# Two-layer diffusion trunk on one core: w_out half loaded during the RWKV recurrence, expert weights in 512 KB pieces, second expert product transposed

## The reference

```python
mix = concat([mla_o, hg_o, rw_o]) @ w_out                    # 1024 x 1024
x   = layernorm(ALPHA * x + g1 * mix) * ln_g[0] + ln_b[0]
h2  = x * (1 + sc2) + sh2
aff = softmax(h2 @ router)                                   # 16 experts
gate, idx = top_k(aff.T, cap)     # per expert: 64 sample tokens, 16 prompt tokens
xe  = h2[idx]
he  = silu(xe @ w1) * (xe @ w3)                              # 1024 -> 1024, twice
ye  = (he @ w2) * gate                                       # 1024 -> 1024
ffn = zeros.at[idx].add(ye)
x   = layernorm(ALPHA * x + g2 * ffn) * ln_g[1] + ln_b[1]
```

## Time and profile before

| | before |
|---|---|
| median of 3 runs | 3464.21 us (3459.65 to 3464.31) |
| the profiled execution, its own time | 3468.49 us |
| its span, first to last instruction | 3466.6 us |
| mean granted TensorE clock | 0.907 of full speed |
| TensorE busy (matmul) | 2812.5 us, 81% of the span |
| VectorE, ScalarE, GpSimd busy | 1260.2, 519.7, 753.1 us |
| moved by DMA | 533.90 MB, mean 154 GB/s |
| expert weight issues (SP) | 128 of 2048 KB, 128 of 1024 KB |

### The profile page before, as it was taken

One profiled execution on the slowest core, in us unless ns is written; L12 is line 12 of the kernel. 1 busy time (PEld: TensorE's weight loads), 2 busy tenths in 40 slices (PEclk: granted clock), 3 DMA queues, 4 the chain that ended last, 5 costly groups with the idle time before them and its releaser, 6 DMA issues. The chain is left out here.

```text
span 3466.6 us, 72945 instructions
## 1 busy us (share of the span) xinstructions
PE 2812.5 (81%) x32720; PEld 1898.1 (55%) x32720; DVE 1260.2 (36%) x2711; ACT 519.7 (15%) x1001; POOL 753.1 (22%) x874
## 2 busy tenths in 40 slices
PE   5998884648584999999979988566585859999995
PEld 1555554538534766666425645355474446666662
DVE  1101668774524111111240036786754331111114
ACT  0102331131101000000010022302211100100101
POOL 0000908343220000000010037272430200000102
PEclk9999996869896999999989999878798879999998
DMA  8300000000052988888661000000003259899972
GB/s 349 129 20 36 1 8 4 2 7 3 3 218 104 387 332 333 338 341 345 254 260 62 2 36 1 9 3 7 2 3 113 118 212 359 342 350 349 349 291 79
DMA packets 68854, 533.90 MB, mean 154 GB/s; under 512 B 12704, under 2 KB 14560, under 8 KB 32192
## 3 DMA queue, kind: packets, MB, share of 16 engines
q1 hardware_dynamic: 65472, 518.75, 38.5%
q0 software_dynamic: 3072, 10.49, 1.1%
HBM read 520.43 MB, written 8.78 MB: 153 GB/s over the span
## 5 line engine op out<-in xcount | busy, mean ns | idle before, releaser
L2276 PEld LDWEIGHTS ps<-arena 128*64 128x64 f32 x16384 | 580.7, 138 | 93.2 <-issue 90.6
L2276 PE MATMUL ps<-arena 128*64 128x80 f32 x16384 | 601.5, 235 | 20.5 <-issue 11.7
L2289 PE MATMUL ps<-arena 128*128 128x512 f32 (+1 forms) x1024 | 472.8, 606 | 4.6 <-ACT arena L2339 4.6
L527 PE MATMUL ps<-arena 128*128 128x128 f32 (+1 forms) x1088 | 294.7, 434 | 4.6 <-DVE arena L580 4.6
L2404 DVE TENSOR_TENSOR arena<-arena,ps 128x32 f32<-128x32 f32 (+1 forms) x192 | 45.1, 263 | 686.0 <-ACT arena L2347 686.0
L2289 PEld LDWEIGHTS ps<-arena 128*128 128x128 f32 (+1 forms) x1024 | 165.2, 171 | 221.3 <-issue 210.4
L527 PEld LDWEIGHTS ps<-arena 128*128 128x128 f32 x1088 | 164.3, 191 | 135.1 <-issue 130.1
L2034 POOL DMA_INDIRECT arena<-h_d,arena x32 | 39.3, 1227 | 800.1 <-DVEq L2371 662.8
L2347 ACT ACTIVATE arena<-ps 128x160 f32<-128x160 f32 x128 | 38.9, 304 | 944.0 <-PE ps L2276 944.0
L2384 DVE TENSOR_TENSOR arena<-arena,ps 128x512 f32<-128x512 f32 x140 | 96.2, 687 | 206.1 <-PE ps L2305 158.2
L1982 PE MATMUL ps<-arena 128*128 128x512 f32 x320 | 141.4, 605 | 25.1 <-DMA arena<-in_w_out 25.1
(11 more groups left out here) (347 smaller groups left out, 4152.9 us busy)
## 6 DMA issues: line engine op xcount, KB each, us to landing
arena<-in_ex_w SPq DMA_DIRECT2D x128, 2048.0 KB, 8.7
arena<-in_ex_w SPq DMA_DIRECT2D x128, 1024.0 KB, 7.6
arena<-in_ada_w SPq DMA_DIRECT2D x24, 2048.0 KB, 13.7
arena<-in_w_t SPq DMA_DIRECT2D x34, 512.0 KB, 3.4
arena<-in_w_out SPq DMA_DIRECT2D x4, 2048.0 KB, 10.3
arena<-in_w_tok SPq DMA_DIRECT2D x2, 3712.0 KB, 17.4
h_d<-x_sb SPq DMA_DIRECT2D x10, 512.0 KB, 2.6
arena<-mod_d SPq DMA_DIRECT2D x8, 512.0 KB, 10.8
```

Source lines behind the costliest of these rows:

```text
L527: i = nc.tensor.matmul(ps[:, n % 8, 0:c1 - c0], ring[:, a % WRING, k, :], e.hT[:, k, c0:c1], start=k == 0, stop=k == KD - 1)
L2276: m = nc.tensor.matmul(gated(j)[c * 64:(c + 1) * 64, f, a, :], w13[:, j, a, k, f * P + c * 64:f * P + (c + 1) * 64], xT[:, x % 2, k, :], s ...
L2289: m = nc.tensor.matmul(ps[0:CAP if x % 2 == 0 else P, 4 + h, :], rows[x % 2][:, f, :], w2[:, (f // 2 + 2) % 4, f % 2, h * 512:(h + 1) * 51 ...
```

## The change

- `w_out` is laid out on the host as [layer, row, half, k, 512]. Its first half is loaded in two pieces by SP within the RWKV phase, after the factor stage (`xy`) and into parts of the arena that the rest of that phase doesn't use (`first_half`). The second half is the first instruction of SP's output program, ahead of `clear_last`.
- A `w1`/`w3` quarter is loaded by four DMAs and a quarter of `w2` by two, each of 512 KB with 4 KB to a partition. There are six slots of 2 MB (`WG`) and four of 1 MB (`WP`). Five quarters are loaded in the output phase; the sixth and four of `w2` in the route phase.
- `project(x, j)` now has `w2` as the stationary side in 128x64 tiles and the 80 tokens as the moving side: 32 matmuls for each quarter, by the same pattern as `gate`. Its result lies with features on partitions. VectorE multiplies it by a g2 column while it copies it out (`weighed`, two instructions for each quarter) to `yS` (sample tokens of a pair) and `yX` (prompt tokens of eight experts).
- `turn_pair` transposes `yS` back with eight 128x128 transposes for each pair, `turn_context` does so with `yX` twice in a layer; ScalarE copies them to `yP` and `yC`. All eight sample blocks of a pair are scattered after quarter 1, behind `turn_tokens`; two prompt blocks follow for each eight experts. Adds go to `x_sb` in place; `yacc`, the memsets and GpSimd's multiplications are gone.
- The prompt tokens' numbers and gates go through DRAM (`ctx_d`) at the end of the route phase and are loaded at the start of the experts phase.
- SP may load the five modulation chunks once the last six gate quarters have freed their slots; the loads follow the last piece of `w2`. norm2 takes `x_sb` where it took `yacc`.

```diff
-        "w_out": f("w_out"), "ln_g": f("ln_g"), "ln_b": f("ln_b"),
+        "w_out": f("w_out").reshape(DEPTH, KD, P, 2, 512).transpose(0, 2, 3, 1, 4), "ln_g": f("ln_g"), "ln_b": f("ln_b"),
         "router": f("router").reshape(DEPTH, KD, P, NE).transpose(0, 2, 1, 3),
         "ex_w13": np.stack([f("ex_w1"), f("ex_w3")], 2).reshape(DEPTH, NE, 2, KD, P, 4, 256).transpose(0, 1, 5, 4, 2, 3, 6),
-        "ex_w2": f("ex_w2").reshape(DEPTH, NE, 4, 2, P, DM).transpose(0, 1, 2, 4, 3, 5),
+        "ex_w2": f("ex_w2").reshape(DEPTH, NE, KD, P, 4, 256).transpose(0, 1, 4, 3, 2, 5),
     }
     out.update(fixed)
...
-    first = ARENA - 12 * 2048
-    slots = [e.part(at, KD, 512)[0] for at in
-             (first + 12288, first + 16384, first + 20480, first + 4096, first)]
+    slots = [e.part(gate_place(FREED_GATES + n), KD, 512)[0] for n in range(RING)]
...
+            sp.wait_ge(S["xy"], LVC * TILES)
+            k = 0
+            for dst in first_half(e):
+                n = dst.shape[1]
+                sp.dma_start(dst, d["w_out"][l, :, 0, k:k + n, :]).then_inc(S["ld_wo0"], 16)
+                k += n
...
+def first_half(e):
+
+    return e.part(e.a1 + 4 * PAD, 6, 512)[0], e.part(e.a0 + 4 * P * TILES, 2, 512)[0]
...
+    wo_a, wo_b = first_half(e)
+    brow, z = e.part(e.a0, 2, DM)
+    gb, z = e.part(e.a0 + 4 * P * TILES + 2 * 512, 2, DM)
+    assert z <= e.a1 + 4 * PAD
+    y, z = e.part(e.a1 + NRW * PAD, 2, DM)
+    wo_1, z = e.part(z, KD, 512)
...
-            e.clear_last(sp)
-            for n in range(2):
-                sp.dma_start(wo[:, n], d["w_out"][l].rearrange("(k p) n -> p k n", p=P)[:, :, n * 512:(n + 1) * 512]
-                             ).then_inc(S[f"ld_wo{n}"], 16)
+            sp.dma_start(wo_1, d["w_out"][l, :, 1]).then_inc(S["ld_wo1"], 16)
             load_gate_rows(e, sp, 0, brow, S["n1ld"])
             load_norm_rows(e, sp, 0, gb, S["n1ld"])
-
-            for j in range(4):
-                load_w13(e, sp, 0, j, mem)
-            for j in (0, 1):
-                load_w2(e, sp, 0, j, mem)
+            e.clear_last(sp)
+
+            for q in range(WG - 1):
+                load_w13(e, sp, q, mem)
...
-                    if t == 0:
-                        pe.wait_ge(S[f"ld_wo{n}"], 16)
+                    if t == 0 and n == 0:
+                        pe.wait_ge(S["ld_wo0"], 32 * (l + 1))
+                    if t == 0 and n == 1:
+                        pe.wait_ge(S["ld_wo1"], 16)
                     for k in range(KD):
-                        m = nc.tensor.matmul(ps[:, 2 * (t % 4) + n, :], e.mixT[:, k, t * P:(t + 1) * P], wo[:, n, k, :],
+                        half = wo_1[:, k, :] if n else wo_a[:, k, :] if k < 6 else wo_b[:, k - 6, :]
...
+WG, WP = 6, 4
+QUARTERS = 4 * NE
+FREED_GATES = QUARTERS - WG
+
+
+def gate_place(q):
+
+    return ARENA - WG * 4096 + (q + 1) % WG * 4096
...
+def load_w13(e, sp, q, mem):
+
+    for a in range(2):
+        for k in range(0, KD, 4):
+            sp.dma_start(mem["w13"][q % WG][:, a, k:k + 4, :].rearrange("p k n -> p (k n)"),
+                         e.d["ex_w13"][e.l, q // 4, q % 4, :, a, k:k + 4, :].rearrange("p k n -> p (k n)")
+                         ).then_inc(e.S[f"ld_e{q % WG}"], 16)
+
+
+def load_w2(e, sp, q, mem):
+
+    for k in range(0, KD, 4):
+        sp.dma_start(mem["w2"][:, q % WP, k:k + 4, :].rearrange("p k n -> p (k n)"),
+                     e.d["ex_w2"][e.l, q // 4, q % 4, :, k:k + 4, :].rearrange("p k n -> p (k n)")
+                     ).then_inc(e.S[f"ld_f{q % WP}"], 16)
 
...
+            sp.wait_ge(S["top"], 1)
+            for n, src in enumerate((pf, val)):
+                sp.dma_start(e.ctx_d[n].rearrange("(e r) -> e r", r=CAPP), src[:, CAPS:CAP]).then_inc(S["ctx_out"], 16)
+            sp.wait_ge(S["ctx_out"], 32)
 
         @block.gpsimd
...
+    HALF = NI // 2
+
+    blocks = [(t, h) for t in range(1, TILES) for h in range(2)]
...
             e.clear_last(sp)
 
-            for j in (2, 3):
-                load_w2(e, sp, 0, j, mem)
-            load_gate_rows(e, sp, 1, brow, S["ld_nb"])
+            for n, dst in enumerate((iC, gC)):
+                for g in range(2):
+                    sp.dma_start(dst[:, g:g + 1], e.ctx_d[n, g * P:(g + 1) * P].rearrange("(p o) -> p o", o=1)).then_inc(S["ld_nc"], 16)
+            for q in range(QUARTERS):
+                if q + WG < QUARTERS:
+                    sp.wait_ge(S["h_ps"], q + 1)
+                    load_w13(e, sp, q + WG, mem)
+                if q >= WP:
+                    sp.wait_ge(S["pr_ps"], q - WP + 1)
+                    load_w2(e, sp, q, mem)
+            sp.wait_ge(S["xe_used"], NE)
             load_norm_rows(e, sp, 1, norm2_rows(e), S["ld_n2"])
             if l + 1 < e.depth:
                 e.mod_l = l + 1
                 for n in range(RING):
-                    if n < 3:
-                        sp.wait_ge(S["h_ps"], 4 * NE - 2 + n)
-                    else:
-                        sp.wait_ge(S["w_used"], 4 * NE - 2 if n == 3 else 4 * NE)
+                    sp.wait_ge(S["h_ps"], FREED_GATES + n + 1)
                     load_chunk(e, sp, n)
             sp.wait_ge(S["ld_n2"], 32)
...
-            def project(x, n):
-
-                f, h = divmod(n, 2)
-                if h == 0 and f % 2 == 0:
-                    pe.wait_ge(S[f"ld_f{f // 2}"], l * (16 * NE) + (x * 16 + 16))
-                    pe.wait_ge(S["he"], 4 * x + f // 2 + 1)
-                if n == 0 and x:
-                    pe.wait_ge(S["ye_sb"], x)
-                m = nc.tensor.matmul(ps[0:CAP if x % 2 == 0 else P, 4 + h, :], rows[x % 2][:, f, :],
-                                     w2[:, (f // 2 + 2) % 4, f % 2, h * 512:(h + 1) * 512], start=f == 0, stop=f == KD - 1)
-                if h and f % 2:
-                    m.then_inc(S["w_used"], 1)
-
-            def scatter(i, k):
-
-                t, h = blocks[k]
-                if k == 0:
...
+            def project(x, j):
+
+                q = 4 * x + j
+                pe.wait_ge(S[f"ld_f{q % WP}"], 32 * (l * NE + x + 1))
+                pe.wait_ge(S["he"], 4 * x + 4)
+                if q >= 2:
+                    pe.wait_ge(S["pr_sb"], q - 1)
+                for b in range(2):
+                    for f in range(KD):
+                        for c in range(2):
+                            m = nc.tensor.matmul(product(j)[c * 64:(c + 1) * 64, b, :],
+                                                 w2[:, q % WP, f, b * P + c * 64:b * P + (c + 1) * 64],
+                                                 he[:, x % 2, f, :], start=f == 0, stop=f == KD - 1)
+                m.then_inc(S["pr_ps"], 1)
+
+            def turn_pair(i):
+
+                pe.wait_ge(S["pr_sb"], 8 * i + 8)
+                if i:
+                    pe.wait_ge(S["sc_ev"], sample_blocks(i))
+                for b in range(KD):
+                    m = nc.tensor.transpose(ps[:, 6 + b // 4, (b % 4) * P:(b % 4 + 1) * P], yS[:, b, :], e.ident[:, :])
+                m.then_inc(S["yt_ps"], 1)
+
+            def turn_context(g):
+
+                pe.wait_ge(S["xe_used"], NI + 2 if g == 0 else NE)
+                for b in range(KD):
+                    m = nc.tensor.transpose(ps[:, b // 4, (b % 4) * P:(b % 4 + 1) * P], yX[:, b, :], e.ident[:, :])
...
+            def scatter(i):
+
+                pe.wait_ge(S["g_sb"], i + 1)
+                pe.wait_ge(S["yt_sb"], 2 * i + 2)
+                for k, (t, h) in enumerate(blocks):
+                    n = sample_blocks(i) + k
+                    if n >= 2:
+                        pe.wait_ge(S["sc_ev"], n - 1)
+                    nc.tensor.matmul(ps[:, 6 + h, :], GP[:, (t - 1) * P:t * P], yP[:, h * 512:(h + 1) * 512],
+                                     start=True, stop=True).then_inc(S["sp_ps"], 1)
...
 
             turn_tokens(0)
             for x in range(NE):
+                i = x // 2 - 1
                 for j in range(4):
                     gate(x, j)
+                    if j == 0 and x % 2 and i >= 0:
+                        turn_pair(i)
+                        if i == HALF - 1:
+                            turn_context(0)
                     if x:
-                        for n in range(4 * j, 4 * j + 4):
-                            project(x - 1, n)
-                    if x % 2 and x >= 3:
-                        for k in range(NB)[spread[j]]:
-                            scatter(x // 2 - 1, k)
-                    if j == 1 and x + 1 < NE:
-                        turn_tokens(x + 1)
-            for n in range(2 * KD):
-                project(NE - 1, n)
-            for k in range(NB):
-                scatter(NI - 1, k)
+                        project(x - 1, j)
+                    if j == 1:
+                        if x + 1 < NE:
+                            turn_tokens(x + 1)
+                        if x % 2 and i >= 0:
+                            scatter(i)
+                            if i == HALF - 1:
+                                scatter_context(0)
```

(70 more changed lines are left out.)

208 lines of the change are left out of this document (93 added, 115 removed).

## The result

The changed kernel takes 3481.24 us (median of 14 runs, 3468.67 to 3492.85), the kernel before beside it 3464.36 (14 runs, 3459.65 to 3468.19): ratio 1.0046, 95% interval 1.0037 to 1.0054. It is slower by 0.46%, where 3268 us had been forecast. The profiled execution has a span of 3474.5 us at a mean clock of 0.907.

A forecast was written before the change was run, and what follows sets the result against it. TensorE was taken to set the experts' pace, with transfers 13% behind; the output phase's start, expert 0 and the tail were bound otherwise. Savings of 100.6 us in layer 0 and 96.7 in layer 1, together 197.3, gave 3268 us, range 3240 to 3335.

The forecast's parts named there:

- The cost of one quarter: Experts phase: a gate and a project quarter together fall from 8.21 to 6.87 us of TensorE time.
- Scatter: Experts phase: eight blocks behind turn_tokens take 8.6 us a pair, the third block waiting for VectorE's first add.
- Start of the experts: Layer 0: 2.1 us from dropped memsets, and expert 0 in 21.1 instead of 24.5 us with weights already in memory.
- Tail: After the last gate: 25.2 us instead of 40.7 and 40.2, a gain of 15.5 and 15.0 us.
- Output phase: Its start: TensorE begins without waiting for w_out, a gain of 11.5 us in layer 0 and 11.8 in layer 1.
- the margin of one microsecond: Output phase start: the second half of w_out is there by 957.1, one microsecond before TensorE needs it.
- experts 1 to 15: Start to end of last gate: 494 us instead of 562.1 and 558.5, saving 68.1 and 64.5, transfers keeping up.
- (1): Rival: the smaller weight pieces bound the experts; at 348 GB/s 20 us a layer more, 3308 us; chance 0.25.
- (3): Rival: each small DMA's fixed cost makes the kernel slower than before, below 303 GB/s; 3518 us at 290; chance 0.04.
- (2): Rival: the output phase's opening doesn't move, only 3.7 us of clears saved in each layer; 3284 us; chance 0.07.
- (4): Rival: VectorE doesn't hold the scatter, 1.7 us less for each of 14 pairs; 3244 us; chance 0.04.

The follow-up runs named there:

- e_open: The kernel before with only the opening of the output phase added (first half of w_out loaded during the RWKV recurrence): 3442.76 us, ratio 0.9939.
- e_free: The changed kernel with all weight transfers still issued, but TensorE reading resident quarters and waiting for no weight after the first two: 3464.68 us (one run).
- e_quiet: The changed kernel loading a third of the weight bytes, with the same instructions and TensorE work: 3258.16 us (one run).
- e_cols: The changed kernel with gate and project matmuls over 40 of the 80 token columns, same instructions and weights loaded: 3545.51 us.
- e_rows4k: The changed kernel with each gate quarter loaded by two 1 MB DMAs keeping 4 KB rows, and each w2 quarter by one: 3503.58 us, ratio 1.0112.
- e_big: The changed kernel with one 2 MB DMA (16 KB rows) for each gate quarter and one 1 MB DMA for each w2 quarter: 3429.03 us, ratio 0.9892.
- e_half_wide: The changed kernel with the second product using 128x128 weights in quarters 1 and 3 and 128x64 in 0 and 2: 3468.41 us, ratio 1.0009.
- e_even_wide: e_big_spread with w2 of the odd experts used in 128x128 weights, in quarters that carry no scatter: 3389.28 us, ratio 0.9775.
- e_big_spread: The changed kernel with whole weight pieces and each pair's scatter dealt out two matmuls to a quarter: 3367.88 us, ratio to the kernel before 0.9709.
- after: The changed kernel itself, as measured and profiled: 3481.24 us, ratio 1.0046 to the kernel before.
- e_two_thirds: The changed kernel loading two thirds of the weight bytes in the experts stage, with the same TensorE instructions: 3400.51 us (one run).

## Why the prediction was wrong

*The cost of one quarter* was right: 6.7 us of TensorE's time, as the clean quarters behind a scatter group show (1461.59 to 1468.28: 6.69; predicted 6.87). *Scatter* was right: third block held by VectorE for 1.23 us, 9.0 us a group against 8.6. *Start of the experts*: 14.0 us earlier = 11.9 + 2.1 as put; expert 0 took 23.4 us instead of 21.1, so that of the 3.4 us put for weights in memory 1.1 came: its gates still stop twice for "issue" (0.56 and 2.48 us). *Tail*: 25.7 us in layer 1 against 25.2, but 29.8 in layer 0, where the loads behind the experts run at 362 GB/s beside it (88 in layer 1) and the products stop twice for "issue" (1.90 and 1.35 us): the same cause as below. *Output phase*: 11.9 and some 11.3 against 11.5 and 11.8, and e_open shows both by themselves. The half matrix in the recurrence costs nothing, and the margin of one microsecond held.

The step that failed is *experts 1 to 15*: 494 us were predicted and 593.9 and 595.9 measured, 99.9 and 101.9 a layer. With the 2.3 and 2.2 of expert 0 that is 206 of the 213 us between 3268 and 3481. The step added up TensorE's work and asked of one supplier only, the weights, if it could follow. With TensorE waiting for no weights at all (e_free) only 5 to 7 us of the 100 come back; with a third of the traffic (e_quiet) all of it does. What TensorE waited for was its own instructions, at the ends of blocks of 256: the stops are a block apart, 60 of the 66 end 1.0 to 1.75 us behind the landing of a block, and with less work in a block the restarts stay 6.3 us apart (e_cols). No run changed the delivery alone, with the traffic as it was.

I had the first sign in hand and misread it. Expert 0 of the kernel before has four gates in a row without projects, and I put its waits down to weights. The 110 records that close end in the middle of a gate, and this is how the same timeline of the kernel before goes on:

```profile
1124.41 4.65 PE L2276 MATMUL ps<-arena 128*64 128x80 f32 x128 [1.35 <-issue]
1131.53 3.71 PE L2276 MATMUL ps<-arena 128*64 128x80 f32 x60 [2.48 <-issue]
```

Two waits marked "issue", 128 records apart. The change made every quarter as dense in instructions as that expert: 192 records in 6.7 us instead of 136 in 8.2. The question that was missed is how many instructions a microsecond the new form issues.

Of the rivals, *(1)* gave the in-stage rate too high still (310 GB/s measured, 348 put), for a reason that isn't its own: the rate follows the stalled TensorE. *(3)* named the turning point rightly, gate 63 being 98.6 us late or a rate under 303 GB/s. Gate 63 was 102 and 104 us late (it starts 612.8 and 614.8 us behind gate 0) and the kernel came out slower; but the mechanism, a fixed cost of each small transfer, is refuted by e_rows4k, which has half as many gate transfers and is slower still. What small pieces do cost is 24 us a layer, by their 4 KB rows. *(2)* and *(4)* didn't happen. One slip of the sum changes nothing: 31 us a layer more is 3330, as rival 1 has it, and not 3328.

The Trainium skill (Runtime: NRT & Kernel Launch, Instruction fetch mechanics) says that engines fetch instructions in 16 KiB blocks of 256 through a DMA queue of their own, and that this is hidden because dispatch is slower than the fill. The blocks and their queue are in this trace. "Hidden" nearly holds for the kernel before at 8.17 us a block (2.6 us idle in 562.1), and for e_quiet at 4.69 (11.4 in 482.7); under weight traffic of 220 to 341 GB/s at 4.6 us of work a block it doesn't, with 96.5 us of idle TensorE in 593.9 in the changed kernel. The Trainium skill's rule on sizes (DMA: Bandwidth & Descriptors, Measured), 1 MiB and more, leans the way of e_big; but e_rows4k has 1 MB transfers and lost.

Open stays: why a block begins to move 3.8 us behind TensorE's restart under the traffic and 1.5 us with little of it (the wait for a DMA engine that is busy with weights, or the memory), and why fewer blocks with more work each gained so little twice (e_half_wide, e_even_wide). Nor is the number of blocks times 6.3 us a law or a floor for the stage: 97 blocks would be 611 us, and e_big_spread takes 561. The 6.3 us hold for the dense quarters in which TensorE waits. Both e_big_spread and e_even_wide move 341 GB/s at a DMA share of 0.9, and there the weights may be as near to binding as the instructions.

## What to carry to other kernels

When an edit makes matmuls smaller and faster, count instructions as well as time: here 256 TensorE instructions (128 small fp32 matmul records with their weight loads) came about 6.3 us apart wherever TensorE waited for them while weights poured in, and 1.3 us saved in a quarter became 0.5 us lost (593.9 us by 60 against 562.1 by 60). Idle time that is marked "issue", in the middle of a run of identical matmuls and always as many records apart, was that limit here, not a late weight. If it can't be avoided, put other work into it: dealing the scatter out over the dense quarters, with large transfers, turned 3481 us into 3368.

## What the runs showed that was not expected

- Weight traffic slows TensorE that waits for no weights: the stage is 104 and 109 us longer in e_free than in e_quiet. Of the 111 us between after and e_quiet two thirds are still there at 220 GB/s (e_two_thirds).
- TensorE goes on 1.4 us behind the landing of its instruction packet, with all the traffic (310 to 341 GB/s) as with less (137).
- fp32 matmuls of 80 columns: with 128x64 weights in alternating halves 36 ns a record, with 128x128 weights 115 ns (128 records in 14.41 us in the tail of e_even_wide are 113), so one wide matmul costs 1.6 times the two narrow ones. With 40 columns instead of 80 the narrow ones take 29 ns a record (128 in 3.75 us).
- An increment of a semaphore as an instruction of its own costs TensorE 79 ns in a stream of matmuls.
- With 40 columns (e_cols) the granted clock was 0.70 and 0.69 in experts 1 to 15 of the two layers, where it was 0.98 and 0.97 with 80, at the same instructions and bytes.
